# Fourth block of the feed-forward and gate stages in the PSUM banks of the token statistics; side factor in SBUF; stream store waited for later

## The reference

```python
h = rms_norm(x, g_ffn_pre[l])
up = h @ w_up[l]
gate_h = causal_dwconv(up[..., :D_FF], ffn_conv_w[l], ffn_conv_b[l])
hid = jax.nn.gelu(gate_h) * up[..., D_FF:]
x = x + rms_norm(hid @ w_down[l], g_ffn_post[l])

ple_gate = jax.nn.sigmoid(rms_norm(x, g_ple_gate[l]) @ w_ple_gate[l])
ple = rms_norm(p[l].astype(x.dtype) @ w_ple_proj[l], g_ple_post[l])
x = x + ple_gate * ple
```

## Time and profile before

| | |
|---|---|
| median of 3 runs | 3326.47 us (3319.42, 3326.47, 3327.20) |
| the profiled execution's own time | 3320.58 us |
| its span, first to last instruction | 3318.8 us |
| mean granted clock of TensorE | 0.990 |
| TensorE matmuls, busy | 3168.1 us (95%) |
| VectorE, ScalarE, GpSimd, busy | 1548.4, 746.6, 1128.2 us |
| HBM read and written | 188.27 and 17.83 MB |

### The profile page before, as it was taken

The page is one execution under the profiler, slowest core; times in us unless marked ns, Lnnn a source line. Parts: engine busy times, 40 slices in busy tenths (PEclk is TensorE's granted clock), DMA queues, the critical chain, the costliest instruction groups (busy, mean ns, idle before and its releaser), DMA issues.

```text
span 3318.8 us, 41623 instructions
## 1 busy us (share of the span) xinstructions
PE 3168.1 (95%) x17494; PEld 2553.9 (77%) x17494; DVE 1548.4 (47%) x1639; ACT 746.6 (22%) x962; POOL 1128.2 (34%) x525
## 2 busy tenths in 40 slices
PE   7999998999989999999999999999799999999997
PEld 5877876787768788788567788788588888888875
DVE  3134428428842431924667701443654055155476
ACT  1011225212221122511235500122210011000241
POOL 2232220125533323034223444453233434434442
PEclk9999999999989999999999999999999999999998
DMA  6200101333131001112021111112211111111211
GB/s 237 70 32 14 39 34 47 126 102 121 57 126 39 14 32 51 55 44 108 33 82 45 39 51 55 38 51 95 82 38 51 45 51 51 44 51 47 102 48 63
DMA packets 59243, 208.15 MB, mean 63 GB/s; under 512 B 5857, under 2 KB 7649, under 8 KB 59105
## 3 DMA queue, kind: packets, MB, share of 16 engines
q1 hardware_dynamic: 42240, 143.15, 13.1%
q10 hardware_dynamic: 16864, 62.97, 5.0%
HBM read 188.27 MB, written 17.83 MB: 62 GB/s over the span
## 4 chain that ended last, share of the span: by engine, by line
PE 80%; DVE 15%; ACT 2%; DMA 2%; issue 1%; ACTq 0%; DVEq 0%
PE ps L545 69%; DVE Sb L1789 3%; PE ps L804 2%; DVE C L1991 1%; PE ps L970 1%; DMA modfirst<-modw 1%; DVE stage L1880 1%; PE ps L572 1%; PE ps L527 1%; PE ps L714 1%; PE ps L629 1%; DVE Y L1875 1%; DMA xin<-xT 1%; DVE stage L1895 1%; DMA x_saved<-Y 0%
## 5 line engine op out<-in xcount | busy, mean ns | idle before, releaser
L471 POOL TENSOR_TENSOR w_hi<-raw,pool_zero 128x1024 fp32r<-128x1024 f32 (+2 forms) x242 | 458.7, 1896 | 2094.6 <-PE ps L545 2017.0
L473 POOL TENSOR_TENSOR w_lo<-raw,w_hi 128x1024 fp32r<-128x1024 f32 (+2 forms) x242 | 634.5, 2622 | 19.0
L545 PE MATMUL ps<-g_hi,w_hi 128*128 128x512 f32 x1536 | 483.4, 396 | 33.7 <-DVE fft L2126 12.2
L545 PE MATMUL ps<-h_hi,w_hi 128*128 128x512 f32 (+1 forms) x1832 | 491.4, 364 | 24.7 <-ACT QK L1125 15.0
L545 PE MATMUL ps<-g_lo,w_hi 128*128 128x512 f32 x1536 | 475.2, 391 | 0.0
L545 PE MATMUL ps<-g_hi,w_lo 128*128 128x512 f32 x1536 | 474.9, 390 | 0.0
L545 PE MATMUL ps<-h_hi,w_lo 128*128 128x512 f32 (+1 forms) x1832 | 470.2, 352 | 0.0
L545 PE MATMUL ps<-h_lo,w_hi 128*128 128x512 f32 (+1 forms) x1832 | 470.1, 352 | 0.0
L545 PEld LDWEIGHTS ps<-h_hi,w_hi 128*128 128x128 f32 x1832 | 301.5, 189 | 97.8 <-issue 22.1
L545 PEld LDWEIGHTS ps<-g_hi,w_hi 128*128 128x128 f32 x1536 | 288.4, 189 | 104.3 <-issue 21.1
L545 PEld LDWEIGHTS ps<-h_hi,w_lo 128*128 128x128 f32 x1832 | 298.6, 189 | 49.8
(11 more groups left out here) (319 smaller groups left out, 3432.7 us busy)
## 6 DMA issues: line engine op xcount, KB each, us to landing
raw<-s SPq DMA_DIRECT2D x226, 512.0 KB, 3.5
modring<-modw ACTq DMA_DIRECT2D x32, 512.0 KB, 4.9
xin<-xT ACTq DMA_DIRECT2D x1, 5120.0 KB, 18.2
x_saved<-Y ACTq DMA_DIRECT2D x1, 5120.0 KB, 16.5
xin<-x_saved ACTq DMA_DIRECT2D x1, 5120.0 KB, 17.5
modfirst<-modw SPq DMA_DIRECT2D x4, 1024.0 KB, 10.8
modfirst<-modw ACTq DMA_DIRECT2D x4, 1024.0 KB, 19.2
x_saved<-Y ACTq DMA_DIRECT2D x1, 4096.0 KB, 11.7
```

What stands on the lines that cost most here:

```text
L471: G.tensor_tensor(w_hi[s][:, :n], raw[s][:, :n], zero.to_broadcast([P, n]), ALU.add).then_inc(hi_done, 1)
L473: G.tensor_tensor(w_lo[s][:, :n], raw[s][:, :n], w_hi[s][:, :n].bitcast(F32), ALU.subtract)\
L545: last = T.matmul(ps[:, o + c0:o + c0 + size], wt[s][:, kk], xx[:, k, t0:t0 + size], start=(x == 0 and n == 0), stop=(x == k_n - 1 and n = ...
```

## The change

At A the filler before slab 4 is 8 instead of 20, ScalarE waits for the store ahead of the first evacuation into `VT`, and store and reload leave out the context columns. At B slab 3 goes to banks 4 and 5, waits for the copied token factor instead of for an evacuation, and VectorE reads it there. At C the same is done with slab 3; the side block's sums and factor are made in banks 2 and 3, the sums behind slab 3 and the factor behind the second step of slab 4; ScalarE copies it to SBUF (`side_scaled`), slab 5 waits for that copy, the eight products with it are taken one by one in the blocks, and the gate input of n + 3 stands behind block n. The loop over slabs 4 to 7 of the gate stage is written out.

```diff
             def slab(g, s, hi, lo, k_n, segs, slot, ready=None, first=False, between=None, order=None, bank=None, idle=0,
+                     scaled=None):
-                if not first:
+                if scaled is not None:
+                    pe.wait_ge(scale_ready, scaled)
+                elif not first:
                     pe.wait_ge(evac_done, g - 1)
...
-                        keep_busy(2, (10, 0, 1, 0, 20, 0)[c])
+                        keep_busy(2, (10, 0, 1, 0, 8, 0)[c])
...
-                    slab(gf + 3, 1, g_hi, g_lo, KD, SEC, 2)
+                    slab(gf + 3, 1, g_hi, g_lo, KD, SEC, 2, bank=4, scaled=1)
...
-            def ple_scale(k):
-                if k == 4:
-                    token_means(5, fft[:])
+            def side_means(k):
                 if k == 7:
-                    spread_inverse(5, 4)
+                    pe.wait_ge(evac_done, G_PLEG + 2)
+                    token_means(5, fft[:], 2)
+            def side_scale(k):
+                if k == 1:
+                    spread_inverse(5, 2)
             slab(G_PLEG + 2, 0, g_hi, g_lo, KD, SEC, 2, first=True, bank=6, between=gate_scale)
-            slab(G_PLEG + 3, 1, g_hi, g_lo, KD, SEC, 2, between=ple_scale)
-            with pe.Fori(2, 4) as j:
-                for s in range(2):
-                    slab(j * 2 + (G_PLEG + s), s, g_hi, g_lo, KD, SEC, 2)
+            slab(G_PLEG + 3, 1, g_hi, g_lo, KD, SEC, 2, bank=4, scaled=2, between=side_means)
+            slab(G_PLEG + 4, 0, g_hi, g_lo, KD, SEC, 2, first=True, between=side_scale)
+            slab(G_PLEG + 5, 1, g_hi, g_lo, KD, SEC, 2, scaled=3)
+            for n in range(6, KD):
+                slab(G_PLEG + n, n % 2, g_hi, g_lo, KD, SEC, 2)
+        side_scaled = C2[:, 8, :]
...
-                if l:
-                    act.wait_ge(xs_out, 16)
...
+                if l:
+                    act.wait_ge(xs_out, 16)
                 for c in range(3):
                     evac(g0 + 6 + 2 * c, VT[:, c, :], T1, 3)
...
-                    act.dma_start(x_saved.rearrange("k p t -> p k t"), Y[:]).then_inc(xs_out, 16)
+                    act.dma_start(x_saved.rearrange("k p t -> p k t")[:, :, CTX:], Y[:, :, CTX:]).then_inc(xs_out, 16)
...
-                if n == 2:
-                    roots(21)
+                if n == 3:
+                    roots(21, 2)
+                    keep_scale(5, side_scaled, 2)
                 act.wait_ge(evac_done, G_PLEG + n + 1)
                 A.activation(gates[n % 3], gates[n % 3], ACT.Sigmoid).then_inc(gate_ready, 1)
...
+                    bv = 4 * BANK if g == G_FFN + 2 else 2 * BANK
-                    V.tensor_tensor(fft[:], ps[:, 2 * BANK:4 * BANK], ffc[:], ALU.mult).then_inc(evac_done, 1)
+                    V.tensor_tensor(fft[:], ps[:, bv:bv + SEQ], ffc[:], ALU.mult).then_inc(evac_done, 1)
...
+            dve.wait_ge(stat_used, 21)
+            gate_input(2)
             inverse_columns(7)
-            gate_input(2)
-            dve.wait_ge(rs_ready, 5)
+            dve.wait_ge(scale_ready, 3)
             for n in range(KD):
-                own.link(V.scalar_tensor_tensor(C2[:, n, :], C2[:, n, :], vcol("g_ple_post", n), ps[:, 4 * BANK:6 * BANK],
+                own.link(V.scalar_tensor_tensor(C2[:, n, :], C2[:, n, :], vcol("g_ple_post", n), side_scaled,
                                                 ALU.mult, ALU.mult))
-            def gated(n):
                 dve.wait_ge(gate_ready, n + 1)
                 own.link(V.tensor_tensor(C2[:, n, :], C2[:, n, :], gates[n % 3], ALU.mult))
                 V.tensor_tensor(B2[:, n, :], B2[:, n, :], C2[:, n, :], ALU.add).then_inc(out_ready, 1)
-            for n in range(3):
-                gated(n)
-            for n in range(3, KD):
-                gate_input(n)
-                gated(n)
+                if n + 3 < KD:
+                    gate_input(n + 3)
```

More of the change, by code:

```diff
@@ L528, in keep_busy, with slab @@
                              start=True, stop=True)
-            def slab(g, s, hi, lo, k_n, segs, slot, ready=None, first=False, between=None, order=None, bank=None, idle=0):
-                if not first:
+            def slab(g, s, hi, lo, k_n, segs, slot, ready=None, first=False, between=None, order=None, bank=None, idle=0,
+                     scaled=None):
+                if scaled is not None:
+                    pe.wait_ge(scale_ready, scaled)
+                elif not first:
                     pe.wait_ge(evac_done, g - 1)
@@ L1008, in _, with token_means @@
                 slab(G_PMIX + 4 * j + 3, 1, r_hi, r_lo, 4, SEC, 2)
-            def token_means(m, total):
+            def token_means(m, total, bank=4):
                 pe.wait_ge(sq_added, m)
                 for t in range(SEQ // P):
-                    last = T.matmul(ps[:, 4 * BANK + t:4 * BANK + t + 1], total[:, t * P:(t + 1) * P], ones[:, 0:1],
+                    last = T.matmul(ps[:, bank * BANK + t:bank * BANK + t + 1], total[:, t * P:(t + 1) * P], ones[:, 0:1],
                                     start=True, stop=True, skip_group_check=True)
@@ L1393, in conv_tiles @@
                         act.wait_ge(conv_done, 4)
-                        act.dma_start(xin[:], x_saved.rearrange("k p t -> p k t")).then_inc(xr_in, 16)
+                        act.dma_start(xin[:, :, CTX:], x_saved.rearrange("k p t -> p k t")[:, :, CTX:])\
+                            .then_inc(xr_in, 16)
                 highs("y1", KD, lambda x: Y[:, order[x], cs], lambda x: h_hi[:, order[x], cs], conv_tiles)
@@ L1516, in _, with roots @@
                 square(n, C2[:, n, :])
-            def roots(used):
+            def roots(used, bank=4):
                 act.wait_ge(stat_used, used)
-                A.activation(rc[:, 0, :], ps[:, 4 * BANK:4 * BANK + 8], ACT.Sqrt, bias=vcol("eps", 1)).then_inc(std_ready, 1)
+                A.activation(rc[:, 0, :], ps[:, bank * BANK:bank * BANK + 8], ACT.Sqrt, bias=vcol("eps", 1)).then_inc(std_ready, 1)
             roots(17)
@@ L1528, in _, with keep_scale @@
             roots(18)
-            def keep_scale(n):
+            def keep_scale(n, dst=token_scale[:], bank=4):
                 act.wait_ge(rs_ready, n)
-                A.activation(token_scale[:], ps[:, 4 * BANK:6 * BANK], ACT.Copy).then_inc(scale_ready, 1)
+                A.activation(dst, ps[:, bank * BANK:(bank + 2) * BANK], ACT.Copy).then_inc(scale_ready, 1)
             keep_scale(2)
@@ L2160, in gate_input @@
                 dve.wait_ge(evac_done, G_PLEG + n)
-                b = 6 * BANK if n == 2 else n % 2 * 2 * BANK
+                b = {2: 6, 3: 4}.get(n, n % 2 * 2) * BANK
                 V.tensor_tensor(gates[n % 3], ps[:, b:b + SEQ], token_scale[:], ALU.mult).then_inc(evac_done, 1)
```

## The result

| | before | after |
|---|---|---|
| median of 4 runs | 3323.05 us (3319.42 to 3327.20) | 3289.32 us (3287.44 to 3290.33) |
| span of the profiled execution | 3318.8 us | 3288.5 us |
| mean granted clock of TensorE | 0.990 | 0.993 |

The ratio is 0.9897, 95% interval 0.9880 to 0.9915: 34 us (28 to 40) off 3323. The forecast was 3291 us, from 3281 to 3302.

A forecast was written before the change was run, and what follows sets the result against it. The chain of waits, four fifths TensorE, was taken to bound the kernel. 17.9 + 6.1 + 8.5 = 32.5 us off gave 3288.1 (profiled execution) and 3294.0 (median), middle 3291 us, range 3281 to 3302.

The forecast's parts named there:

- A: Head of the second layer: slab 4 starts 17.9 us earlier, 7.6 from twelve fillers, the rest the store wait and its clock.
- B: First feed-forward group: slab 3's 12.21 us stall goes, a 6.8 us one comes before slab 4; gain 6.1 us.
- C: Last gate stage: TensorE done 16.3 us earlier, the end 7.8 us longer; gain 8.5 us.
- rival 1: Second-layer weights come late because transfer engines are full; price 4 us, 3295 us; chance 0.06.
- Rival 4: At B slab 4 is held by VectorE's product with slab 3, so B gives nothing: 3297 us; chance 0.05.
- rival 6: At C a table switch costs the skill's 2.66 us, not 1.28: C gains 7.1, time above 3292 us; chance 0.03.
- Rival 2: VectorE sets the pace at C and TensorE waits slab by slab, up to 5 us: 3296 us; chance 0.10.
- rival 3: New gaps of 6.8 and 1.9 us cost 3.1 and 3 us of lower clock: 3295 us; chance 0.14.
- Rival 5: Removing twelve fillers drops TensorE to 1.2 GHz at the second layer's head; six slabs so give 3352 us; chance 0.02.

The follow-up runs named there:

- the wide store: Kernel after with store and reload of the stream at full width again, late wait and 8 fillers kept: 3291.67 us, ratio 0.9899 to before.
- C alone: Kernel after with the changes at A and B taken back, so only the gate stage changed: 3312.13 us, ratio 0.9965 to before.
- 20 fillers: Kernel after with twenty fillers instead of eight ahead of slab 4 of the second layer's first projections: 3297.48 us, ratio 0.9914 to before.
- none: Kernel after with no filler ahead of slab 4 of the second layer's first projections: 3282.88 us, ratio 0.9870 to before.
- the new order: Kernel after with VectorE's gate inputs 5, 6 and 7 moved down in the gate stage's order: 3279.77 us, ratio 0.9867 to before.
- the old wait: Kernel after with ScalarE's store wait back ahead of the QK evacuations, narrow store and 8 fillers kept: 3294.58 us, ratio 0.9907 to before.
- the fillers at the sums: Kernel after with two short fillers ahead of the column sums of the gate stage's second and fourth steps: 3287.84 us, ratio 0.9890 to before.
- A alone: Kernel before with only the change at A (late store wait, narrow store and reload, 8 fillers): 3306.5 us, ratio 0.9942 to before.
- B alone: Kernel before with only the change at B (slab 3 of the first feed-forward group in banks 4 and 5): 3317.75 us, ratio 0.9981 to before.
- the waits for the own banks: Kernel after with slabs 4 and 5 of the first feed-forward group waiting for evacuation of slabs 0 and 1: 3280.65 us, ratio 0.9866 to before.
- all together: Kernel after with no filler ahead of slab 4, VectorE's new gate-stage order and the own-bank waits: 3267.71 us, ratio 0.9829 to before.
- all together with fillers: The kernel of all together plus two fillers ahead of the gate stage's sums: 3268.33 us, ratio 0.9826 to before.

## Why the prediction was right

**A, 17.9 predicted, 18.4 in the pair.** Slab 4 starts 18.97 us behind slab 2's first matmul (19.1 predicted). The twelve fillers were put at 7.6 and are 7.74. The other 10.3 are 10.6: 6.9 for the later wait and 3.7 for the narrower store. The prediction used the narrower store only to say when the transfers end; with the wait moved it buys nothing, as the wide store shows. The weights were in time (rival 1): no wait for GpSimd stands ahead of slab 4, even with no filler.

**B, 6.1 predicted, 6.5 in the pair, 6.3 alone.** All three of its parts came: the idle time 6.74 (6.8), the subtraction that meets GpSimd 3.02 (3.1), and slab 4, which takes 2409.04 - 2396.04 = 13.0 us where an undisturbed slab takes 10.9, so 2.1 for the clock (2.4); the granted clock was 0.52 in its first 4 us and 1.00 behind them. Rival 4 is out: the wait did count slab 2's evacuation alone, and slab 4 was not held by slab 3's. What the prediction did not ask is whether slab 4 needs that wait at all. It does not: waiting for slab 0 is enough.

**C, 8.5 predicted, 7.3 in the pair, 9.1 by the spans with C alone.** TensorE's gain was put at 16.3 and is 16.4, the longer end at 7.8 and is 7.5. The new wait in slab 4 is 1.37, not 1.9: the spread starts 3230.20 - 3224.06 = 6.1 us behind the sums (6.4 predicted), and TensorE is there for it after 4.8 (4.5 predicted). The table load is 1.28 us again, and the root starts at 3229.64, 0.02 after it. The sigmoid ahead of it ends at 3228.32 and the load starts at 3228.34, so no drain stands on either side. The Trainium skill's 2.66 us (ScalarE: Activation LUTs, What ACT_TABLE_LOAD costs) is not borne out here, and rival 6 falls. Rival 2, VectorE's pace, falls with the last inputs' brackets: VectorE waits 1.94, 3.26 and 5.94 us for TensorE.

**Where a term was missing.** Slab 2 of the gate stage took 1.6 us more than in the profile of before. The sum has no such term; rival 3 looked for the lower clock in the new gaps and falls: the gap of 6.74 cost 2.1, and behind that of 1.37 the granted clock was 1.00. The lower clock came ahead of them. No run shows it to be a cost of the change: in the 14 kernels profiled, sums to spread is 6.0 us in seven (before, C alone, 20 fillers, none, the new order, the old wait, the fillers at the sums) and 7.6 in seven (after, A alone, B alone, the wide store, the waits for the own banks, all together, all together with fillers). The edits do not sort them.

**Rival 5** (the fillers held the clock) was given 0.02 and is excluded: every filler more is slower, to none at all.

**The time.** 32.5 was predicted, and the medians are 34 apart. The pair of profiles is only 30.3 apart, since the profiled execution of before (3320.58) lies low among runs that go from 3319 to 3329 us, and that of after carries 1.3 us at A and 1.6 at C of lower clock. Taking the middle between the profiled time and the median kept that error at half its size: the median of 17 runs of before in the first batch was 3324.89. That 32.5 and 34 lie so close is partly chance: the interval is 28 to 40, and the terms missed in both directions (A 0.5 more, B 0.4 more, C 1.2 less in the pair).

## What to carry to other kernels

When a buffer moves, go through every wait that names an owner by its place in an order ("the slab two before"), those that a longer stall has covered too: part of the stall here moved on to a slab whose banks had long been free, and naming the right owner brought 8.7 us, more than the move itself had (6.3). When work is handed to an engine late in a stage, write down what stands behind its last input: three blocks stood there, 7.5 us, and another order of the same work took them back. Fillers are work on the path until a run without them says otherwise; here all twenty ahead of slab 4 were. The program's other fillers, but for the two tried at the sums, were left as they are, and nothing is shown of them.

## What the hardware showed that I had not expected

TensorE's clock falls in places where the program did not change. Windows (us; busy time of each engine; then granted clock, DMA share, GB/s) of the same stretch ahead of place A, of the kernel before and of after:

```profile
600.00:625.00 25.00, 22.14 (x201) 17.50 (x200) 5.85 (x22) 3.82 (x12) 0.00 (x0) 1.00 0.39 142
```

```profile
600.00:625.00 25.00, 22.14 (x183) 17.39 (x180) 5.50 (x22) 3.64 (x10) 0.00 (x0) 0.86 0.34 127
```

TensorE is busy for the same time in both, but was granted 1.00 and 0.86 and did 18 matmuls fewer. TensorE's idle times around the fall are the same in both timelines (0.85, 0.81 and 0.71 us), and GpSimd's next split, which waits for the slab behind them, starts at 626.40 and 628.55. The filler at A, ahead of which no kernel was changed, stood at 951.63 in before and anywhere from 949.28 to 953.26 in the others: 4 us that belong to nobody's edit. In the gate stage, the ten microseconds from the sums on, with C alone, with all gains, and with all gains and fillers ahead of the sums:

```profile
3225.19:3235.19 10.00, 10.00 (x60) 8.81 (x61) 3.62 (x4) 6.17 (x8) 0.58 (x1) 1.00 0.19 54
```

```profile
3185.60:3195.60 10.00, 10.00 (x53) 8.73 (x54) 2.65 (x3) 4.55 (x6) 0.00 (x0) 0.83 0.17 52
```

```profile
3187.83:3197.83 10.00, 10.00 (x53) 8.70 (x54) 2.65 (x3) 4.54 (x6) 0.00 (x0) 0.83 0.16 52
```

TensorE is never idle in any of them. The wait ahead of the sums does not decide: with 1.51 us of it the clock held with C alone and fell with all gains, with 0.22 us it held with the fillers at the sums (6.02 us) and fell with all gains and fillers (7.62). The Trainium skill (TensorE: Matmul & The Clock Gate, Loop structure matters more than you think) has the clock fall when matmuls wait; these four are not sorted by that. The fall follows sixteen one-column matmuls, but with C alone it follows the same sixteen at 1.00. What decides stays open: no run here shifted one stage by a few tenths of a microsecond and left the rest. What it means for reading: profiles with the same instructions and nearly the same waits just ahead of such a place differ by 1.6 us there. Each kernel has one profile here, so that two of one kernel would differ as much is likely but not shown. A gain of that size needs the runs, not the pair.
